# Shares of the projection pieces among the steps of an HGRN head, one list for each number of pieces

## The reference

```python
for l in range(DEPTH):
    u = rmsnorm(h, norm_g[l]).astype(dtype)
    p = u @ w_in[l]
    hq, hf_f, hf_b, hi, hgt, aq, ak, av, agt = jnp.split(p, split_idx, axis=-1)
    o_h = hgrn2_mixer(hq, hf_f, hf_b, hi, hgt, lbs[l], hg_norm_g[l])
    o_a = diff_attention_mixer(aq, ak, av, agt, diff_lambda[l], diff_subln_g[l], l, cos, sin)
    mixed = jnp.concatenate([o_h, o_a], axis=-1).astype(dtype)
    h = h + mixed @ w_out[l]
out = rmsnorm(h, final_norm_g).astype(dtype)
```

## Time and profile before

| | us |
|---|---|
| median of 3 runs | 1478.92 (1478.47 to 1479.08) |
| the profiled execution, its own time | 1478.92 |
| its span, first to last instruction | 1477.1 |
| PE busy | 1463.6 (99%) |
| DVE busy | 1084.6 (73%) |
| ACT busy | 826.8 (56%) |

### The profile page before, as it was taken

The page is one execution under the profiler, slowest core; times in us unless marked ns, Lnnn a source line. Parts: engine busy times, 40 slices in busy tenths (PEclk is TensorE's granted clock), DMA queues, the critical chain, the costliest instruction groups (busy, mean ns, idle before and its releaser), DMA issues.

```text
span 1477.1 us, 27771 instructions
## 1 busy us (share of the span) xinstructions
PE 1463.6 (99%) x11060; PEld 1388.9 (94%) x11060; DVE 1084.6 (73%) x1811; ACT 826.8 (56%) x1754; POOL 106.2 (7%) x110
## 2 busy tenths in 40 slices
PE   9999999999999999999999999999999999999998
PEld 9999999999999999999999999999998889999987
DVE  6887787787665777777667778777886657777754
ACT  7565555665434655655555555566654436665554
POOL 0001110011100000000000010000001000000010
PEclk9999999999999999999999999999999999999999
DMA  5221121121223222222232121211212232222221
GB/s 196 80 64 58 44 73 58 58 72 58 73 69 91 72 73 73 73 73 70 61 101 87 58 71 60 72 58 58 72 58 86 67 107 73 73 73 86 74 84 72
DMA packets 34560, 109.92 MB, mean 74 GB/s; under 512 B 4864, under 2 KB 4992, under 8 KB 34432
## 3 DMA queue, kind: packets, MB, share of 16 engines
q1 hardware_dynamic: 34432, 108.15, 23.5%
HBM read 97.38 MB, written 2.10 MB: 67 GB/s over the span
## 4 chain that ended last, share of the span: by engine, by line
PE 85%; DVE 7%; ACT 4%; issue 3%; DMA 0%; SPq 0%; DVEq 0%; ACTq 0%
PE proj L1652 57%; PE pair L1784 5%; PE far L1899 4%; PE pair L1884 2%; PE pair L1886 2%; PE far L1913 2%; PE far L1901 1%; PE pair L1835 1%; PE far L1770 1%; PE far L1752 1%; ACT q_level L878 1%; PE far L1792 1%; PE far L1854 1%; PE pair L1842 1%; PE far L1855 1%
## 5 line engine op out<-in xcount | busy, mean ns | idle before, releaser
L1652 PE MATMUL proj<-u_hi,w_hi 128*128 128x264 f32 (+1 forms) x2024 | 484.9, 311 | 2.5 <-DVE w_lo L1132 1.2
L1652 PE MATMUL proj<-u_hi,w_lo 128*128 128x264 f32 (+1 forms) x2024 | 458.7, 298 | 0.0
L1652 PE MATMUL proj<-u_lo,w_hi 128*128 128x264 f32 (+1 forms) x2024 | 458.5, 298 | 0.0
L1652 PEld LDWEIGHTS proj<-u_hi,w_hi 128*128 128x128 f32 x2024 | 322.4, 189 | 15.0 <-issue 1.6
L1652 PEld LDWEIGHTS proj<-u_hi,w_lo 128*128 128x128 f32 x2024 | 321.5, 188 | 10.8
L1652 PEld LDWEIGHTS proj<-u_lo,w_hi 128*128 128x128 f32 x2024 | 321.9, 188 | 7.5
L1132 DVE TENSOR_TENSOR w_lo<-w_raw,w_hi 128x1024 fp32r<-128x1024 f32 x178 | 219.6, 1234 | 49.4 <-ACT w_hi L720 49.4
L945 ACT ACTIVATE decay<-pair,neg_max 128x528 f32<-128x528 f32 (+1 forms) x144 | 100.4, 697 | 218.1 <-DVE neg_max L1511 218.0
L720 ACT ACTIVATE w_hi<-w_raw 128x1024 fp32r<-128x1024 f32 x178 | 186.6, 1049 | 43.2 <-PE proj L1652 40.5
L1511 DVE TENSOR_REDUCE neg_max<-pair 128x1 f32<-128x528 f32 (+1 forms) x144 | 101.5, 705 | 110.5 <-PE pair L1886 110.4
L1784 PE MATMUL pair<-q_level,qk_dec 128*128 128x128 f32 x768 | 104.5, 279 | 2.8 <-ACT q_level L878 2.5
(11 more groups left out here) (237 smaller groups left out, 2356.1 us busy)
## 6 DMA issues: line engine op xcount, KB each, us to landing
w_raw<-w_units SPq DMA_DIRECT2D x178, 512.0 KB, 3.5
q_stack<-gate_f SPq DMA_DIRECT2D x32, 132.0 KB, 2.4
k_stack<-k_stack SPq DMA_DIRECT2D x32, 132.0 KB, 2.4
h<-x_t SPq DMA_DIRECT2D x8, 264.0 KB, 5.2
cos_sin<-rope SPq DMA_DIRECT2D x2, 528.0 KB, 5.8
out_t<-ops SPq DMA_DIRECT2D x2, 512.0 KB, 3.5
out_t<-decay SPq DMA_DIRECT2D x2, 512.0 KB, 3.9
masks<-level_masks SPq DMA_DIRECT2D x1, 448.0 KB, 6.1
```

Of the source, the lines that this page charges most:

```text
L1652: ins = pe.matmul(out, w, x[:, tile, cols_n], start=(k == 0 and p == 0), stop=(k == last_k and p == 2))
```

## The change

`HG_FEED` becomes a table with a list for each number of pieces, each with that number as its sum, so that nothing is rounded:

```diff
-HG_FEED = (2, 4, 5, 3, 3, 3, 3, 3, 3, 3, 3, 3, 2)
+HG_FEED = {39: (2, 4, 5, 3, 3, 3, 3, 3, 3, 2, 3, 3, 2), 40: (2, 4, 5, 3, 3, 3, 3, 3, 3, 3, 3, 3, 2),
+           35: (2, 4, 5, 3, 3, 3, 3, 2, 2, 2, 2, 2, 2)}
...
-    shares = HG_FEED if c < HG_HEADS else AT_FEED if c < HEADS - 1 else LAST_FEED
+    shares = HG_FEED[len(fed_pieces(c))] if c < HG_HEADS else AT_FEED if c < HEADS - 1 else LAST_FEED
```

## The result

The changed kernel takes 1482.01 us (median of 9 runs, 1480.48 to 1485.1); the kernel before, on the same chip, 1479.00 (median of 9, 1478.47 to 1479.24). By the medians that is 3.0 us slower than before, and 2.3 above the forecast of 1479.7; the ratio over all runs is 1.0024 [1.0015, 1.0032], a little more than that of the medians, because the high runs weigh in it. The nine times lie in clusters some 1.5 us apart: 1480.48, 1480.49, 1480.89; 1481.86, 1482.01; 1483.5, 1483.64; 1484.95, 1485.1. The mean granted clock falls with them, from 1.000 in the first cluster to 0.996 in the last. Runs of the kernel before, 1478.47 to 1479.24, have no such clusters. (The mean covers the whole execution.

What follows compares the result with a forecast made beforehand. TensorE was taken as the bound, busy 1463.6 of 1477.1 us, so only waits could move. Saving 3.9 us in heads 0 to 2 and losing 4.7 in head 7 gave + 0.8: 1479.7 from 1478.92, range 1476.8 to 1482.6.

Steps and rivals of the forecast that it cites:

- Heads 0 to 2: Both layers: one piece more in step 6 removes TensorE's waits at steps 7 and 8, saving 3.9 us.
- The addition of 0.24 to each named idle time: Heads of 39 pieces: real loss taken as the profile's idle time plus 0.24 us, since 0.27 named was 0.51 lost.
- Head 7 up to step 10: Waits of steps 7 and 8, 0.65 us, exchanged for one of 0.9 at step 8: 0.2 worse a layer.
- Head 7, step 12, layer 0: Evacuation and low cut of `av` now precede `chain_forward`, so TensorE waits about 2.5 us: 2.3 us worse.
- I take 2.4: Layer 1, head 7: step 12 waits for the same chain, with the same added VectorE work; 2.4 us worse.
- the far end of 1.60: Head 7: longest time allowed for the low cut of `av`, 1.60 us; the mean, 1.23, was taken.
- The sum at full clock: Whole kernel: 3.9 us saved in heads 0 to 2, 4.7 lost in head 7, + 0.8 together.
- A fall to 1.2 behind the new wait: Head 7, both layers: rival, clock drops to 1.2 GHz, some 5 us more, 1484.7; chance 0.04.
- The bounds of the terms: Whole kernel: bounds of saving and loss together give - 1.2 to + 2.5 us, before widening.
- A: Rival, head 7: VectorE's evacuation and low cut find a gap, no long wait at step 12; 1473.8, chance 0.09.
- B: Rival, heads 0 to 2: the waits turn up again in step 9 behind ScalarE's copies; 1483.6, chance 0.11.

Runs made afterwards that it cites:

- e7_late_round: The changed kernel with ScalarE's rounding of `mixed` in layer 1, head 7, one step later, so `mix_lo` does not run beside the low cut; 1481.97 us.
- e4_late_evac_and_cut: The changed kernel, but in head 7 both the evacuation of `av` and its low cut stand behind `chain_forward`; 1476.78 us.
- e3_late_cut: The changed kernel, but in head 7 the low cut of `av` stands behind `chain_forward`, its evacuation still ahead; 1478.01 us.
- e2_only35: The kernel before with only head 7's part of the change, heads 0 to 2 keeping their old counts; 1487.78 us.
- d3_wait_24: The kernel before with three spare VectorE products in head 7, step 10, ahead of `stack_low`, no piece moved; 1486.37 us.
- d5_wait_38: The kernel before with five spare VectorE products in head 7, step 10, ahead of `stack_low`, no piece moved; 1491.01 us.
- d2_wait_16: The kernel before with two spare VectorE products in head 7, step 10, ahead of `stack_low`, no piece moved; 1482.85 us.

## Why the prediction was right or wrong

**Heads 0 to 2: right.** - 3.9 predicted, - 3.91 measured, in each head within 0.02. The addition of 0.24 to each named idle time, the point that the bounds did not cover, held.

**Head 7 up to step 10: right.** Heads 0 to 2 bring everything forward by 0.71 + 0.75 + 0.71 = 2.17. Put back, step 8's level starts at 370.54 + 2.17 = 372.71 (forecast 372.6), after a wait of 0.68 named, 0.92 by distance (0.9). Steps 7 and 8 together lose 0.24 and 0.29 (0.2). The backward products are at 376.29 + 2.17 = 378.46 (379.4 - 1.06 = 378.34).

**Head 7, step 12, layer 0: right.** `chain_forward` begins 381.96 - 377.38 = 4.58 behind `chain_back` (4.7, less some overlap), step 12 another 1.73 later (1.73). It starts at 383.69 + 2.17 = 385.86 against 385.6. The loss is 2.5 where 2.3 was put: 0.12 from the backward products, the rest since only 0.12 of overlap, not 0.3, came off the 4.7.

**Layer 1: mis-sized.** The term "I take 2.4" measured 2.9. The low cut took 1.58 beside GpSimd's `mix_lo`, which the sum entered with the mean of 178, 1.23; the far end of 1.60 would have been right here. The kernel before has `mix_lo` in layer 1 beside `chain_forward` (1114.59, 1.29 us), and its low cut, at 1117.89, took 1.22; the change brought the two together. From L1419 to L1426 are 1117.64 - 1113.03 = 4.61 in layer 1 and 381.96 - 377.71 = 4.25 in layer 0, and e7_late_round shows the 0.37 directly. The other 0.1 to 0.2 is not traced to an instruction. The row with 1.60 had the sign of it: GpSimd's `mix_lo` was at work then too, from 383.94 to 385.70.

**The sum at full clock** was + 0.8 predicted and + 1.5 measured: 0.2 from layer 0, 0.5 from layer 1.

**The clock: priced, and all but dismissed.** "A fall to 1.2 behind the new wait" had a chance of 0.04. By the clusters it came in six of the nine runs, in one to three stretches, and makes half of the median's + 3.0. Its size was put too high, 2.5 us a layer where one stretch costs 1.6 (the 5 us at 1.2 GHz behind it came from no row), its likelihood far too low: that no wait of the trace before is as long as 2.5 was taken as no evidence either way, and then given the smallest of all chances. The Trainium skill, "TensorE: Matmul & The Clock Gate", section "HAM oscillation — how this bites in real kernels", holds that idle gaps between bursts of matmuls can bring the gate down. The runs agree that a gap can do it: the granted clock was 0.58 over the four microseconds behind one of 2.43 us. They go further than the page, whose gaps are longer.

That a gap of given length does not decide alone is seen in e7_late_round, where the clock fell behind 2.42 and not behind 2.43. What decides in a given run stays open.

**The total: in part luck.** The median of 1482.01 lies within the stated 1476.8 to 1482.6, but not for the reasons given. The bounds of the terms ended at + 2.5, 1481.4; the rest of the range was added for partial forms of A and B, and neither came about. What carried the median there is the clock, whose fall the range was not meant to cover, and four of the nine runs lie above the range. The mechanism of both terms was right, and 1480.5, the time at full clock, is what they account for.

## What to carry to other kernels

A step gets room by giving up a piece of filler, but what was to hide behind that filler moves too: here the small waits of six heads went as planned, and one unit that landed a step earlier put 1.9 us of VectorE's work ahead of a chain that TensorE waits for, twice. Before a unit's landing is moved, look at what stands behind its evacuation and cut on the same engine. And where a change makes one long TensorE wait out of nothing (here 2.4 us and more), price the clock as well as the wait.

## What the runs showed of the hardware

- The clock falls behind a single wait in the middle of otherwise dense work. With waits of up to 0.7 and 1.3 us (e4_late_evac_and_cut, e3_late_cut), no run of 11 and 11 shows a cluster of its own. By the times of the runs, with 1.4 and 2.4 it fell in 4 of 9, with 2.4 and 2.8 in 6 of 9 (the changed kernel) and 5 of 5 (e2_only35), with 2.2 and 3.2 and with 3.6 and 4.7 in 5 of 5.
- In the traced runs it fell behind waits of 2.42 (e7_late_round), 2.43 (the changed kernel, layer 0), 2.8 (e2_only35), 3.2 (d3_wait_24), 3.6 and 4.7 (d5_wait_38), and not behind 1.4 and 2.4 (d2_wait_16), 2.2 (d3_wait_24), 2.4 (e2_only35, layer 0), 2.43 (e7_late_round, layer 0) and 2.79 (the changed kernel, layer 1). Between 2.4 and 2.8 it went either way.
- A stretch at 1.2 GHz was 3.4 us long and cost 1.6 (step 12 of layer 0: + 3.84 with it, + 2.22 in e7_late_round without); d5_wait_38 had 6.8 in one layer. Such a stretch costs less where part of it lies in the wait: in layer 1 of e7_late_round it began 0.4 us ahead of the first matmul, and head 7 gave + 3.9 there, where + 2.9 less the 0.37 of the low cut was to be expected at full clock, an estimated 1.4.
- The start of the fall is not always behind the end of the wait: after, the granted clock is still 1.00 from 383.8 to 383.9 and the first matmuls follow 0.31 apart (383.69 to 384.00), the next 0.43; in e7_late_round the clock is 0.50 from 1116.7, within the wait, and already the first, at 1117.10, are 0.58 apart. At full clock they are 0.29 apart (382.70 to 382.99, e3_late_cut).
- VectorE's two-input instructions can take longer beside GpSimd's: the low cut from 1.22 to 1.58 us, two half-height products from 1.43 to 2.41; GpSimd's own from 1.30 to 1.76 or 1.57. The Trainium skill, "GPSIMD Engine Reference", section "Specifications", states that GpSimd shares its SBUF interfaces with VectorE and contends with VectorE instructions that have two SBUF inputs. The trace agrees, by these numbers.
